# The last head of each layer routed for two tiles on one load, and gathers handled in groups of two picks

## The chip, the cores and the metric

One core of one Trainium2 chip runs the whole program in a single launch. The metric is device time in microseconds (us), on the only core, as a median of runs. Below, TensorE, VectorE, ScalarE, GpSimd and SyncE stand in the profile as PE, DVE, ACT, POOL and SP.

## What is computed

Two layers of a decoder trunk over 256 tokens of width 1024, all float32. Each layer first mixes tokens (attention with a forget gate, a pooling mixer and a state-space mixer beside each other), then applies a retrieval layer (PEER) over 16384 experts. The second part, cut to what matters here:

```python
def peer_ffn(h, w_q, sub_keys, u_tab, v_tab):
    q = einsum('bsd,de->bse', h, w_q).reshape(bsz, s, 8, 2, 128)
    scores = einsum('bshid,hikd->bshik', q, sub_keys)
    top_s, top_i = top_k(scores, 16)                      # for each half
    cand = top_s[..., 0, :, None] + top_s[..., 1, None, :]
    best_s, best_j = top_k(cand.reshape(..., 256), 16)
    experts = i1 * 128 + i2                               # 16 for each of 8 heads
    gates = softmax(best_s)
    act = gelu(einsum('td,tkd->tk', hh, u_tab[experts]))
    return einsum('tk,tkd->td', gates * act, v_tab[experts])
```

So every token needs 8 x 16 = 128 experts, and each expert is a row of 1024 numbers of u and 1024 of v (8 KB).

## The kernel before, in words

The 256 tokens are two tiles of 128, one token in each partition. With two layers that makes four steps (STEPS): steps 0 and 1 are tiles 0 and 1 of layer 0, steps 2 and 3 those of layer 1. A **pick** is one of a token's 128 experts. For each pick `gather` has POOL issue one indirect DMA, which brings 128 rows of 8 KB into one of SLOTS = 13 slots (L583). DVE multiplies the u half with the token's activations and sums (`dots`, L1427). ACT applies Gelu and the gate and scales a small diagonal matrix with the result (`weigh`, L931, L938, L947). PE multiplies this diagonal with the v half into PSUM (`add_last`, L1830). Only then is the slot free, and POOL, which waits for `expert_done`, issues the gather that is 13 picks further on.

Picks go in groups of GRP = 4 (a "quad", QUADS = 32 in a step). `dots` of a group run at its `open`, `weigh` at its `close`, and PE adds a group at the `close` of the following one.

While the picks of step n are worked off, the engines also compute the token mixing of step n + 1 and its **routing**. Routing one head takes: `rp`, 16 matmuls of the query projection (L1752); a copy by ACT (L890); `route`, two matmuls for the scores (L1791); a copy by ACT (L917); and on DVE two rounds of top 16 that end with the expert numbers (L1392) and the gates (L1365); `soft` on ACT is the softmax in between. All engines follow one list, `ORDER`, built by `script()`: the rows of MIX, MIX1 and ROUTES are dealt out evenly over the quads of the step before them, `while at < len(rows) * (quad + 1) // QUADS`. In step 0 there are 33 rows for 32 quads, so quad 31 has two: route6 and route7 of tile 1. MIX0 is the order of the start, before any expert can be gathered.

The weights come in blocks (chunks). The 12 blocks of tile 0's token mixing lie in the slots at first. All others pass through a ring of two buffers (`RING`, L518 on SP); the block for c waits until block c - 2 has been used. A routing block holds a head's projection and keys, 1152 KB. Each tile loads its own: RING has 60 blocks. `hT` holds the transposed activations that `rp` reads; step n + 1 overwrites them.

```python
            for c, (n, i) in enumerate(RING):
...
                if c >= 2:
                    sp.wait_ge(S["chunk_used"], uses(*RING[c - 2]))
                w = width(i)
                sp.dma_start(ring[:, c % 2, 0:w], weights[n // TILES, i, :, 0:w])
```

Of the kernel before, what the change touches and what calls it, by code (L numbers as in the profile page):

```python
# [23 lines left out]
P = 128  # L24
# [18 lines left out]
GRP = 4  # L43
# [21 lines left out]
for _name, _w in (("g1", 8), ("fbias", 1), ("qg", 1), ("kg", 1), ("pscale", 2), ("dskip", 2), ("glub", 2), ("og", 8),  # L65
# [40 lines left out]
ROUTES = tuple((f"route{h}",) for h in range(1, PH))  # L106


def script():
# [6 lines left out]
    for n in range(STEPS):  # L116
        if n == 0:

            rows = [(1, r) for r in ((), ("qkn",), ("qkT", "v"))]
            rows += [(0, r) for r in ROUTES[1:]] + [(1, r) for r in MIX1]  # L120
        else:
            rows = [(n + 1, r) for r in MIX + ROUTES] if n + 1 < STEPS else []
# [14 lines left out]
    for quad in (QUADS, QUADS + 1):  # L137
        order += [("open", n, quad), ("close", n, quad)]
# [11 lines left out]
def chunk_order():  # L150
# [7 lines left out]
    return order  # L158


USES = chunk_order()
RING = [c for c in USES if not in_slot(*c)]


# [1804 lines left out]
```

## Time and profile before

| | |
|---|---|
| time, median of 3 runs | 1546.36 us (1545.2 to 1547.12) |
| the profiled execution's own time | 1547.98 us |
| its span, first to last instruction | 1546.1 us |
| busy in the span: PE, DVE, ACT, POOL | 68%, 70%, 37%, 40% |
| moved by DMA | 623.55 MB, of these 536.90 MB by the gathers' queue |
| mean granted TensorE clock | 0.826 of 2.4 GHz |

The profile names an instruction by its line, its engine, what it writes and reads, and gives busy time, the mean length and the idle time of the engine just before it. A group of rows by stretch gives, from left to right, the stretch, its length, the busy time of PE, of PE's weight loads, of DVE, ACT and POOL, each with the count of instructions, then the granted clock, the busy share of the 16 DMA engines (it can pass 1 a little) and the GB/s they moved.

### The profile page before, as it was taken

The page shows a single profiled execution, that of the slowest core. Times are in us where ns is not written, and L with a number is a line of the kernel's source. Part 1 is how long each engine was busy: PE and PEld are TensorE (multiplying, and loading weights), DVE is VectorE, ACT ScalarE, POOL GpSimd, SP SyncE. Part 2 cuts the span into 40 slices and gives each one's busy share as a digit, 9 for nine tenths or more (in the row PEclk, how much of TensorE's full clock was granted, in tenths as well). Part 3 has the DMA queues.
Part 4 walks back from the last instruction along what each step waited for, and adds up shares of the span by engine and source line. Part 5 has one row for each costly group of instructions (what it writes and reads, how often), then busy time and mean ns, then how long its engine had stood idle before and what let it go on. Part 6 is the DMA issues. An engine that isn't in the chain of part 4 may idle for free. (4 is left out here: it accounts for less than half of the span.)

```text
span 1546.1 us, 19439 instructions
## 1 busy us (share of the span) xinstructions
PE 1049.1 (68%) x6790; PEld 532.8 (34%) x6790; DVE 1083.2 (70%) x2485; ACT 575.1 (37%) x1768; POOL 619.7 (40%) x571
## 2 busy tenths in 40 slices
PE   8898656785854668776775667788588465565555
PEld 6685312333531334332552334333255111111111
DVE  8777998646999685654789767564579965444444
ACT  5544433623444433441544431354234432221222
POOL 0034345442753533443343433444243354455441
PEclk9999877887986988787897788889698777667767
DMA  9289999999999999999999999999999999999997
GB/s 381 89 326 421 420 421 420 421 421 405 422 421 368 411 422 421 421 421 421 409 421 421 421 421 421 421 422 420 422 386 421 421 421 422 421 421 422 421 421 304
DMA packets 86642, 623.55 MB, mean 403 GB/s; under 512 B 10000, under 2 KB 10128, under 8 KB 11792
## 3 DMA queue, kind: packets, MB, share of 16 engines
q0 software_dynamic: 73728, 536.90, 83.7%
q1 hardware_dynamic: 12816, 85.41, 13.4%
q8 instruction: 53, 0.87, 0.2%
q14 instruction: 45, 0.37, 0.1%
HBM read 621.23 MB, written 1.05 MB: 402 GB/s over the span
## 5 line engine op out<-in xcount | busy, mean ns | idle before, releaser
L583 POOL DMA_INDIRECT slots<-experts,idx x512 | 593.2, 1159 | 886.5 <-PE psum L1830 709.9
L1427 DVE CUSTOM_DVE_ANT_0 slots<-slots,h 128x1024 f32<-128x1024 f32 x512 | 615.9, 1225 | 390.8 <-DMA slots<-experts,idx 387.6
L1830 PE MATMUL psum<-slots,diag 64*64 64x512 f32 x4088 | 599.3, 737 | 312.4 <-ACT diag L947 312.3
L1830 PEld LDWEIGHTS psum<-slots,diag 64*64 64x64 f32 x4088 | 175.8, 165 | 684.2 <-ACT diag L947 368.9
L931 ACT ACTIVATE ge<-ge 128x4 f32<-128x4 f32 x130 | 26.7, 205 | 437.3 <-DVE ge L1427 436.3
L1752 PE MATMUL psum<-hT,ring 128*128 128x128 f32 x992 | 131.3, 297 | 20.7 <-DMA ring<-weights 16.0
L931 ACT ACT_TABLE_LOAD x55 | 70.6, 1283 | 194.7 <-DVE ge L1427 194.3
L947 ACT ACTIVATE diag<-cst,ge 128x64 f32<-128x64 f32 x511 | 136.5, 336 | 6.7 <-PE psum L1830 2.5
L1752 PEld LDWEIGHTS psum<-hT,ring 128*128 128x128 f32 x992 | 127.7, 212 | 23.5 <-issue 17.7
L938 ACT ACTIVATE ge<-ge,gate 128x1 f32<-128x1 f32 x512 | 109.1, 283 | 4.2
L1525 PE MATMUL psum<-ring,hT 128*128 128x256 f32 x192 | 52.2, 433 | 17.5 <-DVE work L981 17.5
L1525 PEld LDWEIGHTS psum<-ring,hT 128*128 128x128 f32 x192 | 41.1, 220 | 31.3 <-DVE work L981 19.2
L1699 PE MATMUL psum<-ring,work 128*128 128x512 f32 x96 | 44.4, 605 | 0.0
L1427 DVE DVE_READ_ACCUMULATOR2_ANT ge<- 128x1 f32 x512 | 42.1, 82 | 0.0
L925 ACT ACT_TABLE_LOAD x30 | 38.5, 1283 | 0.5
L1791 PE MATMUL psum<-ring,work 128*128 128x128 f32 x124 | 22.5, 305 | 15.8 <-ACT work L890 15.8
L890 ACT COPY work<-psum 128x256 f32<-128x256 f32 x31 | 11.5, 372 | 58.2 <-PE psum L1752 54.6
L809 ACT ACT_TABLE_LOAD x12 | 15.4, 1283 | 43.4 <-DVE att_s L1232 43.4
L1791 PEld LDWEIGHTS psum<-ring,work 128*128 128x128 f32 x124 | 16.6, 194 | 40.4 <-ACT work L890 22.1
L1738 PE MATMUL psum<-cst,h 128*128 128x128 f32 x24 | 5.9, 427 | 30.7 <-DVE h L1295 30.7
L1699 PEld LDWEIGHTS psum<-ring,work 128*128 128x128 f32 x96 | 17.3, 190 | 24.8 <-issue 24.8
L1539 PE MATMUL psum<-work,c_bar 128*32 128x128 f32 x64 | 5.0, 386 | 28.6 <-DVE work L981 28.6
(292 smaller groups left out, 1075.4 us busy)
## 6 DMA issues: line engine op xcount, KB each, us to landing
ring<-weights SPq DMA_DIRECT2D x32, 1152.0 KB, 10.0
ring<-weights SPq DMA_DIRECT2D x26, 1024.0 KB, 9.2
slots<-weights SPq DMA_DIRECT2D x11, 1024.0 KB, 20.0
slots<-experts,idx POOLq DMA_INDIRECT x512, 20.8
ring<-weights SPq DMA_DIRECT2D x2, 1056.0 KB
sml<-small SPq DMA_DIRECT2D x2, 652.0 KB, 9.1
slots<-weights SPq DMA_DIRECT2D x1, 1056.0 KB, 9.0
xs<-x SPq DMA_DIRECT2D x2, 512.0 KB, 13.2
```

The costliest lines, as they stand in the source:

```text
L583: pool.indirect_dma_start(out=slot[:, place(E), :], out_offset=None, in_=src, in_offset=bass.IndirectOffsetOnAxis(ap=idx[:, n % 2, e:e + 1 ...
L809: told(act.activation(prob[:, h % 2, 0:w], PX[:, h % 2, 0:w], ACT.Exp, bias=att_s[:, 0, h:h + 1], accum_out=att_s[:, 1, h:h + 1]), "exp_re ...
L925: told(act.activation(bs[:, 1, :], bs[:, 0, :], ACT.Exp, bias=rs[:, 0:1], accum_out=rs[:, 1:2]), "gexp_ready")
L931: told(act.activation(ge[:, 1, G % 2, :], ge[:, 0, G % 2, :], ACT.Gelu_apprx_tanh), "gelu_ready")
L938: ins = act.activation(ge[:, 2, G % 2, i:i + 1], ge[:, 1, G % 2, i:i + 1], ACT.Copy, scale=gate[:, n % 2, e:e + 1])
L947: act.activation(diag[:, d % DIAGS, :], c_("fold"), ACT.Copy, scale=ge[:, 2, G % 2, i:i + 1]).then_inc(S["diag_ready"], 1)
L1427: ins = dve.tensor_tensor_reduce(u, u, h2[:, n % 2, :], 1.0, 0.0, ALU.mult, ALU.add, d[:, i:i + 1])
L1525: ins = pe.matmul(bank[:, (i % 2) * 256:(i % 2) * 256 + 256], hT_(n)[:, k, :], c[:, k, :], start=(k == 0), stop=(k == KD - 1))
L1699: ins = pe.matmul(out_at(n, i)[:, half, :], merged(n, k), c[:, (k % 2) * D + half * 512:(k % 2) * D + half * 512 + 512], start=(k == first ...
L1752: ins = pe.matmul(PB[:, 2 + h % 2, i * P:i * P + P], c[:, k, i * P:i * P + P], hT[:, k, :], start=(k == 0), stop=(k == KD - 1))
L1791: ins = pe.matmul(PB[:, 2 + h % 2, 256 + i * P:256 + i * P + P], qTs[:, h % 2, i * P:i * P + P], raw[:, KD * 256 + i * P:KD * 256 + i * P ...
L1830: ins = pe.matmul(acc[HALF * half:HALF * half + HALF, i, :], diag[rows, d % DIAGS, :], slot[rows, place(E), D + half * 512:D + half * 512 ...
```

## The change

1. **Groups of two.** GRP is 2, so a step has 64 quads. The last two picks of the last step stay single as before.
2. **One load for two tiles.** Head 7 (SHARED) of the two tiles of a layer is routed one directly after the other from one block. `owner` names both by one ring entry, and `given_back` lets the buffer go after the second. RING has 58 blocks. So tile 0's head 7 is routed only after tile 1's token mixing, and tile 1's heads go in the order 7, 0, 1, ... 6. Both tiles' transposed activations must exist then, so odd steps keep theirs in the work buffer W[0] (`hR_`).
3. **Placing.** `rows_of` gives even steps a first part (until quad EARLY = 46: the rest of the own routing, the mixing of the next tile) and a second (9 routings in the last 18 quads). No quad has two routings.
4. **`adds`.** In front of the rows that hold one of FOLLOWS, PE adds the group that waits, instead of behind the row.
5. **The start.** MIX0 puts `qkn0` before `scan0`, halves `scan0` (`scan_im`), spreads `mul0` to `mul3`, and lets the projections `p`, `qkv0` and `qkv1` of tile 1 go ahead of `route1`. SP loads the block CH_Q before the constants.

```diff
-GRP = 4
+GRP = 2
...
-        "power4", "qkv0", "f", "prep", "fx", "ln", "mul0", "mul1", "mul2", "mul3", "rotate0", "rotate1", "cum", "cm",
-        "qkv1", "rotate2", "bu", "qkv2", "scan0", "qkv3", "qkn0", "scan1", "qkn1", "qkv4", "pool", "qkT", "pre0", "pre1",
...
+        "power4", "qkv0", "f", "prep", "fx", "ln", "mul0", "rotate0", "rotate1", "cum", "cm", "mul1", "mul2",
+        "qkv1", "rotate2", "bu", "qkv2", "qkv3", "qkn0", "scan0", "qkn1", "scan_im", "qkv4", "pool", "qkT", "pre0", "pre1",
+        "mixp", "mul3", "sq1", "scan1", "scan2", "scan3", "scan4", "scan5", "scan6", "logits0", "scan7", "big0", "logits1",
...
+SHARED = (7,)
+OWN = tuple(h for h in range(PH) if h not in SHARED)
+EARLY = (TOPK * SHARED[0] - SLOTS - 7) // GRP
+FOLLOWS = {"normT", "u", "qkv0", "y", "glu", "qkT", "att1", "att2", "att3", "att4", "out0", "h2T"}
+def rows_of(n):
+    if n == STEPS - 1:
+        return [], 0, QUADS
+    pair = [(n + i, h) for h in SHARED for i in range(2)]
...
+    if n % TILES:
+        rows = last_row(rows, n + 1, OWN[0]) + routing([(n + 1, h) for h in OWN])
+        return rows, len(rows), QUADS
+    rows = last_row(rows, n, SHARED[0])
+    late = routing(pair + [(n + 1, h) for h in OWN])
...
+    return rows + late, len(rows), EARLY
...
+                if FOLLOWS.intersection(row):
+                    order.append(("mix", "adds", n))
...
+def owner(n, i):
+    return (n - n % TILES, i) if i - CH_ROUTE in SHARED else (n, i)
-RING = [c for c in USES if not in_slot(*c)]
+RING = list(dict.fromkeys(owner(*c) for c in USES if not in_slot(*c)))
...
+def given_back(n, i):
+    return uses(n + 1, i) if i - CH_ROUTE in SHARED else uses(n, i)
...
+        def hR_(n):
+            return W[0][:, :].rearrange("p (a b) -> p a b", a=KD) if n % TILES else hT
...
             chunk(CH_POOL)
+            chunk(CH_Q)
             sp.dma_start(cst[:, P:], consts[:, P:]).then_inc(S["cst_in"], 16)
...
-                    sp.wait_ge(S["chunk_used"], uses(*RING[c - 2]))
+                    sp.wait_ge(S["chunk_used"], given_back(*RING[c - 2]))
...
+            def adds(n):
+                add_last()
```

How the order moves, at the places that matter. First PE at the end of tile 1's token mixing in step 0, where `out0` to `out3` are L1699, the transposes of `h2T` are L1738, `rp` L1752 and `route` L1791. Before:

```order
160 L1699 MATMUL psum<-ring,work 128x512 x4
161 L1830 MATMUL psum<-slots,diag 64x512 x16
162 L1699 MATMUL psum<-ring,work 128x512 x4
163 L1830 MATMUL psum<-slots,diag 64x512 x16
164 L1738 MATMUL psum<-cst,h 128x128 x8
165 L1752 MATMUL psum<-hT,ring 128x128 x16
166 L1830 MATMUL psum<-slots,diag 64x512 x16
167 L1791 MATMUL psum<-ring,work 128x128 x2
168 L1752 MATMUL psum<-hT,ring 128x128 x16
169 L1830 MATMUL psum<-slots,diag 64x512 x16
```

With the change, the same place (`out3` L1763, `h2T` L1802, `rp` L1814, `route` L1854, adding L1891; a pick is four matmuls in this list, and eight in the profile, which counts each float32 matmul twice):

```order
159 L1763 MATMUL psum<-ring,work 128x512 x4
160 L1891 MATMUL psum<-slots,diag 64x512 x16
161 L1763 MATMUL psum<-ring,work 128x512 x4
162 L1891 MATMUL psum<-slots,diag 64x512 x16
163 L1802 MATMUL psum<-cst,h 128x128 x8
164 L1814 MATMUL psum<-hT,ring 128x128 x16
165 L1891 MATMUL psum<-slots,diag 64x512 x8
166 L1854 MATMUL psum<-ring,work 128x128 x2
167 L1814 MATMUL psum<-work,ring 128x128 x16
```

Between `out3` and `h2T` there are now the adds of two groups of two, up to the group just weighed, where before the group of four weighed during `out3` was added behind `rp`.

Then PE at the end of step 0. Before, and behind it with the change:

```order
183 L1752 MATMUL psum<-hT,ring 128x128 x16
184 L1830 MATMUL psum<-slots,diag 64x512 x16
185 L1791 MATMUL psum<-ring,work 128x128 x2
186 L1752 MATMUL psum<-hT,ring 128x128 x16
187 L1791 MATMUL psum<-ring,work 128x128 x2
188 L1830 MATMUL psum<-slots,diag 64x512 x48
```

```order
187 L1854 MATMUL psum<-ring,work 128x128 x2
188 L1814 MATMUL psum<-work,ring 128x128 x16
189 L1891 MATMUL psum<-slots,diag 64x512 x16
190 L1854 MATMUL psum<-ring,work 128x128 x2
191 L1891 MATMUL psum<-slots,diag 64x512 x48
```

The two `route` with no adds between them (185 and 187 of before) are apart now. Last, DVE at the start, where L1187 is `qkn0`, L1122 the scans, L1210 `big0`, and the rows of 128x1024 around them `scan0` and `qkn1`. Before:

```order
95 L981 TENSOR_TENSOR work<-psum,rot 128x1024 x2
96 L981 TENSOR_TENSOR work<-work,ring 128x1024
97 L981 TENSOR_TENSOR work<-work 128x1024
98 L1187 TENSOR_REDUCE ssqk<-work 128x16
99 L1122 SCALAR_TENSOR_TENSOR work<-decay,work 128x128 x2
100 L1192 RECIPROCAL ssqk<-ssqk 128x16
101 L981 TENSOR_TENSOR work<-psum,ssqk 128x1024
102 L1122 SCALAR_TENSOR_TENSOR work<-decay,work 128x128 x12
103 L1210 TENSOR_REDUCE att_s<-psum 128x4
```

With the change:

```order
95 L1041 TENSOR_TENSOR work<-psum,rot 128x1024 x2
96 L1251 TENSOR_REDUCE ssqk<-work 128x16
97 L1041 TENSOR_TENSOR work<-work,ring 128x1024
98 L1256 RECIPROCAL ssqk<-ssqk 128x16
99 L1041 TENSOR_TENSOR work<-psum,ssqk 128x1024
100 L1041 TENSOR_TENSOR work<-work 128x1024
101 L1186 SCALAR_TENSOR_TENSOR work<-decay,work 128x128 x14
102 L1274 TENSOR_REDUCE att_s<-psum 128x4
```

The normalised queries and keys are written by the instruction numbered 99 now, with one 128x1024 pass and two scans fewer ahead of it.

## Rows read from the trace of the kernel before

**Rows 1.** The page: GB/s in 40 equal slices of the span.

```profile
GB/s 381 89 326 421 420 421 420 421 421 405 422 421 368 411 422 421 421 421 421 409 421 421 421 421 421 421 422 420 422 386 421 421 421 422 421 421 422 421 421 304
```

**Rows 2.** The page: all DMA traffic.

```profile
DMA packets 86642, 623.55 MB, mean 403 GB/s; under 512 B 10000, under 2 KB 10128, under 8 KB 11792
```

**Rows 3.** By stretch: the places with less than full rate; columns as explained above.

```profile
42.00:90.00 48.00, 45.99 (x302) 35.54 (x301) 35.19 (x84) 27.84 (x71) 2.99 (x3) 0.96 0.22 79
376.00:396.00 20.00, 17.64 (x151) 12.08 (x154) 15.22 (x44) 7.66 (x27) 8.30 (x8) 0.99 0.96 392
466.00:476.00 10.00, 7.49 (x44) 2.79 (x48) 9.72 (x33) 4.24 (x13) 4.39 (x4) 0.69 0.70 267
498.00:512.00 14.00, 11.99 (x99) 6.47 (x92) 13.79 (x25) 9.15 (x31) 10.85 (x8) 0.95 0.94 360
750.00:756.00 6.00, 6.00 (x57) 3.81 (x50) 4.14 (x16) 2.53 (x11) 4.18 (x4) 1.00 0.94 365
1122.00:1136.00 14.00, 14.00 (x116) 8.99 (x115) 9.89 (x34) 6.03 (x23) 5.99 (x6) 0.93 0.85 322
1526.00:1546.10 20.10, 10.81 (x72) 2.93 (x64) 10.39 (x16) 4.74 (x19) 0.00 (x0) 0.75 0.48 198
```

**Rows 4.** The page, DMA issues: the routing blocks.

```profile
ring<-weights SPq DMA_DIRECT2D x32, 1152.0 KB, 10.0
```

**Rows 5.** Timeline of the end of tile 1's mixing in step 2: PE (two), POOL.

```profile
1118.20 6.63 PE L1752 MATMUL psum<-hT,ring 128*128 128x128 f32 x32 [1.56 <-ACT hT L880]
1124.76 3.67 PE L1830 MATMUL psum<-slots,diag 64*64 64x512 f32 x32
...
1126.15 1.44 POOL L583 DMA_INDIRECT slots<-experts,idx  x1 [19.66 <-PE psum L1830]
```

**Rows 6.** Timeline: when ACT has the waiting group's diagonals there.

```profile
1116.00 1.06 ACT L947 ACTIVATE diag<-cst,ge 128x64 f32<-128x64 f32 x4
```

**Rows 7.** Timeline of the end of step 0: PE (two), POOL.

```profile
466.66 1.23 PE L1791 MATMUL psum<-ring,work 128*128 128x128 f32 x4 [8.66 <-ACT work L890]
467.82 5.79 PE L1830 MATMUL psum<-slots,diag 64*64 64x512 f32 x32
...
470.11 0.97 POOL L583 DMA_INDIRECT slots<-experts,idx  x1 [13.12 <-PE psum L1830]
```

**Rows 8.** Timeline of DVE: the expert numbers of two consecutive routed heads.

```profile
454.27 0.18 DVE L1392 SCALAR_TENSOR_TENSOR idx<-ex 128x16 uint32<-128x16 f32 x1
467.22 0.17 DVE L1392 SCALAR_TENSOR_TENSOR idx<-ex 128x16 uint32<-128x16 f32 x1
```

**Rows 9.** Gathers issued in 1160 to 1170, 1220 to 1230, 470 to 475: issue to landing.

```profile
DMA to landing us min/median/max: 26.5/28.2/29.1
...
DMA to landing us min/median/max: 13.0/17.6/18.1
...
DMA to landing us min/median/max: 5.5/6.3/9.6
```

**Rows 10.** Timeline of the start: DVE (three), PE (two), ACT.

```profile
18.54 0.25 DVE L981 TENSOR_TENSOR rot<-phase,cst 128x8 f32<-128x8 f32 x2
40.10 1.23 DVE L981 TENSOR_TENSOR work<-psum,ssqk 128x1024 f32<-128x1024 f32 x1
48.01 0.69 DVE L1210 TENSOR_REDUCE att_s<-psum 128x4 f32<-128x512 f32 x1 [2.04 <-PE psum L1601]
...
41.38 1.36 PE L1560 MATMUL psum<-cst,work 128*128 128x128 f32 x8 [3.28 <-DVE work L981]
46.71 1.71 PE L1601 MATMUL psum<-kT,qT 64*128 64x128 f32 x16
...
36.20 1.02 ACT L755 ACTIVATE work<-psum 128x1024 f32<-128x1024 f32 x1
```

**Rows 11.** The page, costliest groups: the Gelu of a group.

```profile
L931 ACT ACTIVATE ge<-ge 128x4 f32<-128x4 f32 x130 | 26.7, 205 | 437.3 <-DVE ge L1427 436.3
```

**Rows 12.** Timeline of the end: DVE's final additions.

```profile
1540.66 3.05 DVE L978 SCALAR_TENSOR_TENSOR xs<-slots,ge,psum 64x512 f32<-64x512 f32 x4 [0.71 <-PE psum L1830]
```

More of the change, by code:

```diff
@@ L103, with routing, last_row @@
         ("att3", "max3", "nrm3"), ("att4", "attg", "sq"), ("merge", "out0"), ("out1", "x1a"),
[2 rows of a table removed]
-ROUTES = tuple((f"route{h}",) for h in range(1, PH))
+        ("out2", "x1p"), ("out3", "x1"), ("h2T",))
+SHARED = (7,)
+OWN = tuple(h for h in range(PH) if h not in SHARED)
+EARLY = (TOPK * SHARED[0] - SLOTS - 7) // GRP
+FOLLOWS = {"normT", "u", "qkv0", "y", "glu", "qkT", "att1", "att2", "att3", "att4", "out0", "h2T"}
+def routing(heads):
+    rows = []
+    for (n, h), ahead in zip(heads, heads[1:] + [None]):
+        rows.append((n, (f"route{h}",) + ((("rp%d" % ahead[1], ahead[0]),) if ahead else ())))
+    return rows
+def last_row(rows, n, h):
+    step, row = rows[-1]
+    return rows[:-1] + [(step, row + ((f"rp{h}", n),))]
+def rows_of(n):
+    if n == STEPS - 1:
+        return [], 0, QUADS
+    pair = [(n + i, h) for h in SHARED for i in range(2)]
+    if n == 0:
+        rows = [(1, r) for r in ((), ("qkn",), ("qkT", "v"))]
+        rows += routing([(0, h) for h in OWN[2:]]) + [(1, r) for r in MIX1]
+    else:
+        rows = [(n + 1, r) for r in MIX]
+    if n % TILES:
[3 more added lines that the diff above has]
+    late = routing(pair + [(n + 1, h) for h in OWN])
+    if n == 0:
+        late = [(step, row + ((f"tab{5 + i - 4}", TILES),) if 4 <= i < 7 else row) for i, (step, row) in enumerate(late)]
+    return rows + late, len(rows), EARLY
 def script():
@@ L116, in script @@
     for n in range(STEPS):
[L117 to L122, printed above, removed]
+        rows, early, until = rows_of(n)
         at = 0
@@ L128, in script @@
             done = at
-            while at < len(rows) * (quad + 1) // QUADS:
+            due = (early * (quad + 1) // until if quad < until else
+                   early + (len(rows) - early) * (quad + 1 - until) // (QUADS - until))
+            while at < due:
                 step, row = rows[at]
-                order += [("mix", s, 2 if s[:3] == "tab" else step) for s in row]
+                if FOLLOWS.intersection(row):
+                    order.append(("mix", "adds", n))
+                order += [("mix", s, step) if type(s) is str else ("mix",) + s for s in row]
                 at += 1
@@ L136, in script @@
                 order += [("mix", "soft" + s[5:], step) for s in row if s[:5] == "route"]
-    for quad in (QUADS, QUADS + 1):
-        order += [("open", n, quad), ("close", n, quad)]
-    return order + [("mix", "drain", STEPS - 1)]
+    return order + [("open", n, QUADS), ("close", n, QUADS), ("mix", "drain", STEPS - 1)]
 ORDER = script()
@@ L158, in chunk_order, with turn_of, routes_before @@
     return order
+def owner(n, i):
+    return (n - n % TILES, i) if i - CH_ROUTE in SHARED else (n, i)
 USES = chunk_order()
-RING = [c for c in USES if not in_slot(*c)]
+RING = list(dict.fromkeys(owner(*c) for c in USES if not in_slot(*c)))
+RSEQ = [(b, int(a[5:])) for kind, a, b in ORDER if kind == "mix" and a[:5] == "route"]
+def turn_of(n, h):
+    return RSEQ.index((n, h))
+def routes_before(stage):
+    return sum(1 for kind, a, b in ORDER[:ORDER.index(stage)] if kind == "mix" and a[:5] == "route")
+def given_back(n, i):
+    return uses(n + 1, i) if i - CH_ROUTE in SHARED else uses(n, i)
 FREE = CH_POOL
@@ L191, in experts_of @@
     start, end = PICKS * n + GRP * quad, PICKS * n + GRP * quad + GRP
-    if start >= PICKS * STEPS:
-        alone = PICKS * STEPS - 2 + quad - QUADS
-        return range(alone, alone + 1)
-    return range(start, min(end, PICKS * STEPS - 2))
+    last = PICKS * STEPS - 1
+    return range(start, min(end, last)) if start <= last else range(last, last + 1)
 BY_VECTOR = {PICKS * STEPS - 1}
@@ L495, in _ @@
             rest_(0)
-            for i in range(6):
+            for i in range(1, 6):
                 chunk(CH_Q + i)
@@ L906, in route @@
             def route(n, h):
-                R = PH * n + h
+                R = turn_of(n, h)
                 if R == 0:
@@ L1116, in scan @@
                     link(tt(w3[0], w3[0], spare, ALU.add))
-                    link(tt(w3[1], w3[1], w3[3], ALU.subtract))
+                if part == 9:
+                    scan_im(n)
                 todo = [(r, b) for r in range(2) for b in range(SB)]
```

58 lines of the change are left out of this document (28 added, 30 removed), and 18 rows, old and new, of tables (MIX, MIX0, MIX1).

## The prediction

> **What bounds the kernel now.** The first view to read is the page's line of GB/s by slice [rows 1]. In most of the 40 slices it stands at 420 to 422, and it never stays above. That is what the DMA engines can do with this traffic, so the kernel is bound by bytes wherever this line is full. At 421 GB/s the 623.55 MB of [rows 2] take 1481 us. The profiled execution took 1547.98 us around a span of 1546.1 us, 1.6 us above the median of the runs, 1546.36 us; I make the sum in differences and take them off the median.
>
> So the second question is where the DMA engines are not full, since only that and the bytes can give time back. The stretches answer it [rows 3]. Each loses its length times (421 - GB/s) / 421. The start, 42 to 90 us, loses 48 x 342 / 421 = 39.0 us: the first weights are in, and no expert can be fetched before the first head is routed. The end loses 20.1 x 223 / 421 = 10.6 us. Between them lie five holes: 1.4 us at 376, 3.7 at 466, 2.0 at 498, 0.8 at 750 and 3.3 at 1122, together 11.2 us. With 1481 that is 1542 of the 1546 us; the rest is mostly the ramp of the first 20 us.
>
> The third view is the timeline at the holes. Those at 376, 750 and 1122 are one pattern. In the last one POOL issues no gather for 19.66 us [rows 5], as no slot comes free: the diagonals of the waiting group of four are there from 1116.0 on [rows 6], but PE works in order and has `h2T` and `rp` first, and `rp` takes 6.63 us at the low clock. The adds follow at 1124.76, the gather at 1126.15. The hole at 466 is another: PE stands 8.66 us before `route` of the doubled quad, while a group of four waits behind it, and then adds at the low clock for 5.79 us [rows 7]. The hole at 498 follows from the second routing of that quad, which keeps DVE from the dots.
>
> **The change, part by part.**
>
> *Bytes.* Two routing blocks of 1152 KB, 1.18 MB each [rows 4], are no longer loaded: 2.36 MB / 421 GB/s = 5.6 us. This counts in full if the DMA engines stay full around it. If VectorE is the bound in those two stretches it counts nothing, which is the other end: 0 to 5.6. I take 5.6, since the line was at 421 through the routing stretches at 1160 to 1240 as well [rows 1].
>
> *The three holes at `h2T`*, 1.4 + 0.8 + 3.3 = 5.5 us. Now PE adds the two groups of two before the transposes, as soon as ACT has the diagonals, so at about 1117 and not 1124.8 in the case of [rows 5, 6]: gathers resume some 8 us sooner and the pause of 19.66 us shrinks to about 12. The hole of 3.3 us needs only 3.3 of these 8. Late next is `h2T`, by the 3.7 us of the adds, and so `rp`; behind `rp` two to four picks wait again. Head 7's `route` stands two quads later, about 5 us, so VectorE doesn't wait for it. I keep 0.5 us of hole: minus 5.0 us (bounds 0 and 5.5).
>
> *The two holes of the doubled quad*, 3.7 + 2.0 = 5.7 us. No quad has two routings now, and every second quad has none, so PE meets adds of two picks between them. In the second hole the DMA share was 0.94 at 360 GB/s, so engines were busy but moved less: the small tables of layer 1 come there, and they still do. I leave 1.5 us: minus 4.2 us (bounds 0 and 5.7).
>
> *The start.* Until the first gather everything hangs on DVE's queue. DVE writes the normalised queries from 40.10 on, PE transposes them at 41.38, has the logits from 46.71 on, and DVE stands 2.04 us until 48.01 [rows 10]. The scan pass and two scans that were ahead go behind, so qkn_ready comes one 128x1024 pass (1.23 us) and two scans of 128 columns (0.74 us) sooner, 2.0 us. The scans that fill the time until the logits are the same work, so DVE's standing goes away, and all behind moves by 2.0 us. ACT must have the squares when DVE is through with `bu`, which is 40.10 less three passes of 1.23, the two scans and a reciprocal, so at 35.4. It began them at 36.20 and took 1.02, behind 32 small multiplications of mul0 to mul3. Eight of them now come later, some 1.8 us, and `f`, which heads the chain, comes sooner with CH_Q loaded first, I take 1 us; so ACT begins at about 33.4 and ends at 34.4, in time. The constants move behind 1 MB, 2.5 us, and DVE first reads them at 18.54, with some us in hand. Tile 1's first projections go ahead of route1, which frees slots 6 to 8 sooner and delays nothing before pick 16. Minus 2.0 us (bounds: plus 1, where a load is late; minus 3).
>
> *A new cost: nine routings in a row.* A routing with its four dots takes DVE 467.22 - 454.27 = 12.95 us [rows 8]. DMA needs 4 gathers of 1.05 MB and a block of 1.18 MB for it, 12.8 us. They are nearly even. Now nine stand in a row in steps 0 and 2, and one of them has no block to load: 9 x 12.95 = 116.6 us of DVE against 112 of DMA. So VectorE falls behind by 4.6 us, where eight of before were behind by 1.5. What covers this is the queue of issued gathers. Its depth is the time from issue to landing [rows 9]: 28.2 us when routing begins at 1160, 17.6 at 1220, and 6.3 in a hole, where it is empty. Groups of two free slots earlier by about two picks' dots, 2.3 us, each time. I expect it to get shallow but seldom empty: plus 1.0 us (bounds 0 and 9, see the rivals).
>
> *More instructions.* ACT has 127 Gelus more, 205 ns each [rows 11], 26 us in all. ACT is 37% busy, and what hides them is the time in which DMA lands the next pick. In the routed stretches they are at most 18 x 0.2 = 3.6 us each on ACT, which isn't the late engine there. DVE and ACT hand over twice as often; between 0 and the same 0.2 us a group, inside the term above. Nothing.
>
> *SP and POOL.* The pair's buffer goes back a routing later, and the next load is wanted two quads after that, as before; at 10.0 us to landing [rows 4] it fits in the 12.95. POOL's three table pieces in step 0 stay behind routings. Nothing. *The end.* DVE's last additions start at 1540.66 [rows 12], after the single picks' last gate value; these stay single. Nothing.
>
> Sum: -5.6 - 5.0 - 4.2 - 2.0 + 1.0 = **-15.8 us**: 1530.6 us for the median (1532.2 for the profiled execution).
>
> **The rivals.**
>
> *B, VectorE drains the queue.* The queue lost 28.2 - 17.6 = 10.6 us in 60 us, 4.6 routings: 2.3 us each [rows 9]. Nine of them and the pair's missing block would take 20.7 + 2.8 = 23.5 of the 28.2 us, and leave 4.7, under the 6.3 of an empty queue. POOL's table work in step 0 and the drain behind both stretches come on top. About 4 us each, 8 in all: 1538.6 us. Against it speaks that last blocks of a layer aren't loaded in that fall, and that groups of two return slots sooner.
>
> *C, the sharing doesn't save what it says.* The block for (1, 0) is loaded late, behind the second use of the shared one, and PE stands before it for 2 us in each layer, or the start doesn't move: 4 us more, 1534.6 us. For: `given_back` is later by one routing. Against: the lead of one routing, 12.95 us, is unchanged.
>
> *D, smaller bursts keep TensorE at its low clock, and it becomes the bound.* At the low level `rp` takes 6.63 us, `route` 1.23 and four picks 5.79 [rows 5, 7], 13.65 us for a routing, against 12.8 us of DMA. Add a wait for the diagonals of two groups, half of the 1.06 us of four picks [rows 6] for each, and it is 14.7. Over the 25 routings that stand close (9 + 7 + 9) that is 25 x 1.9 = 48 us, less what three queues of about 9 us give: +21 beyond the forecast, 1552 us, slower than before. It decides from about 14.6 us a routing on: there 25 times the excess, less 27, eats the 15.8. Against: `rp` and adds still lie end to end, and the clock granted in the full stretches at 376 and 1122 was 0.99 and 0.93 [rows 3]. The Trainium skill has such a rule, in "TensorE: Matmul & The Clock Gate", section "HAM oscillation — how this bites in real kernels": bursts of matmuls that are shorter than the wait before them begin at half rate each time. By that rule the adds of this change, in half the size, would each start cold, and 1552 would be the time. The trace agrees in part: in the stretch of the lone burst at 467.82 the granted clock was 0.69 [rows 3].
>
> *E, nothing to see.* The holes come back elsewhere and VectorE's backlog eats the bytes too: within 3 us of 1546.4.
>
> **How the numbers follow.** The forecast has 0.64, B 0.18, C 0.07, D 0.06, E 0.05. The predicted time is that of the likeliest, 1530.6 us. Its own bounds reach down to 1526 (all holes gone, 3 us at the start) and up to 1535. To hold 8 in 10 the range goes to 1540, which takes in B and C with their spread and leaves out D and E. A measurement here can tell 0.2%, 3.1 us. Faster by more than that are the forecast, B and C, 0.89; within it E, 0.05; slower D, 0.06.
>
> **What would show it.** DMA traffic of 621.2 MB. 421 GB/s in all slices after the third. No pause of POOL over 15 us at the three `h2T`, and landing times that stay over 8 us at the ends of the two long routing stretches. The first gather at 84.3 and not 86.3 us. The forecast is wrong if DVE shows 99% busy there beside DMA slices under 400 (B), if PE stands before L1814 for a block (C), or if a routing takes PE over 13 us (D).

## The result and the profile after

The changed kernel takes **1549.76 us** (median of 20 runs, 1547.69 to 1552.14), the kernel before 1546.36 us beside it (20 runs, 1545.2 to 1548.04): a ratio of 1.002, 95% interval 1.0013 to 1.0027, so 3.4 us more. Forecast were 1530.6 us, and 1525.5 to 1540.0 as range. The profiled execution took 1551.14 us around a span of 1549.3 us.

The page of the changed kernel, bytes, and GB/s by slice, to be held against [rows 1, 2]:

```profile
GB/s 378 91 335 421 420 421 421 386 403 421 421 398 332 423 420 421 421 421 421 422 420 421 420 421 421 421 420 406 421 421 421 412 374 422 421 421 421 421 421 314
DMA packets 86357, 621.22 MB, mean 401 GB/s; under 512 B 9968, under 2 KB 10096, under 8 KB 11760
```

The bytes are the forecast's to the tenth. But the line isn't full: there are dips in slices 8, 9, 12, 13, 28, 32 and 33. The stretches of the changed kernel (start to end, length, busy time and count of PE, PEld, DVE, ACT and POOL, granted PE clock, DMA share, GB/s):

```profile
42.00:90.00 48.00, 45.90 (x294) 35.18 (x293) 36.45 (x86) 29.17 (x78) 3.46 (x4) 0.97 0.25 87
270.00:320.00 50.00, 36.70 (x230) 15.12 (x226) 28.32 (x58) 29.05 (x78) 17.80 (x18) 0.84 0.95 380
376.00:396.00 20.00, 12.03 (x100) 8.08 (x102) 18.22 (x53) 9.72 (x26) 14.46 (x29) 0.92 1.01 422
470.00:500.00 30.00, 14.00 (x80) 4.52 (x84) 27.70 (x85) 12.63 (x35) 7.78 (x8) 0.64 0.80 308
750.00:756.00 6.00, 5.14 (x40) 2.44 (x33) 3.07 (x5) 2.19 (x6) 4.57 (x4) 0.90 1.01 419
1122.00:1136.00 14.00, 10.67 (x88) 6.80 (x90) 12.90 (x44) 7.36 (x21) 3.90 (x4) 0.91 1.01 420
1220.00:1260.00 40.00, 24.44 (x160) 7.19 (x152) 38.18 (x88) 17.68 (x55) 15.39 (x15) 0.72 0.91 366
1526.00:1549.30 23.30, 11.79 (x56) 2.76 (x56) 11.62 (x18) 5.15 (x20) 0.00 (x0) 0.65 0.59 244
```

Three of these places in the kernel before, which [rows 3] doesn't have:

```profile
270.00:320.00 50.00, 40.04 (x235) 18.82 (x232) 32.82 (x65) 30.42 (x84) 20.23 (x19) 0.86 1.01 421
470.00:500.00 30.00, 10.53 (x76) 3.18 (x72) 29.01 (x87) 11.91 (x31) 9.59 (x9) 0.68 0.96 387
1220.00:1260.00 40.00, 19.09 (x140) 5.59 (x136) 33.54 (x76) 13.41 (x45) 20.11 (x18) 0.79 1.01 421
```

The ledger below (us) has each kernel's bytes at 421 GB/s and, by stage, the length times (421 - GB/s) / 421 of stretches of 10 us, added up. Bytes and losses give the span by arithmetic, whatever the kernel. So the ledger says where a span is lost, and not that an edit which closes a hole makes the span shorter by as much. The experiments below are read by it too, each in its one profiled execution, which can lie some 2 us off the median (that of the changed kernel 1.4 above, that of the kernel without `adds` 2.3 below).

| | bytes | start, to 90 | attention rows | `h2T` rows | routing, 400 to 520 | routing, 1150 to 1300 | tail, from 1500 | span |
|---|---|---|---|---|---|---|---|---|
| before | 1481.1 | 42.7 | 0 | 5.6 | 5.7 | 0 | 10.7 | 1546.1 |
| changed | 1475.6 | 42.1 | 6.4 | 0.1 | 10.2 | 5.1 | 9.8 | 1549.3 |
| forecast's change | -5.6 | -2.0 | 0 | -5.0 | -3.2, both routing stretches | | 0 | |

So two terms came in the size forecast (the bytes; the holes at `h2T`, 376, 750 and 1122, which are full now), and two things went against the sum: 6.4 us at the attention rows, which the forecast did not look at, and 9.6 us more in the two long routing stretches, where it had 3.2 us less.

**The attention rows.** Timeline of the changed kernel around two rows of attention of step 1 (computed during step 0) (start, us, engine, line, operation; in brackets the idle time ahead and who ended it), PE, ACT and DVE:

```profile
293.16 5.36 PE L1891 MATMUL psum<-slots,diag 64*64 64x512 f32 x32 [3.61 <-ACT diag L1007]
...
299.04 0.70 PE L1644 MATMUL psum<-kT,qT 64*128 64x256 f32 x2
...
294.66 0.59 ACT L1007 ACTIVATE diag<-cst,ge 128x64 f32<-128x64 f32 x2
...
287.75 0.42 DVE L1296 TENSOR_REDUCE att_s<-psum 128x1 f32<-128x256 f32 x1 [4.05 <-PE psum L1646]
...
295.06 1.22 DVE L1491 CUSTOM_DVE_ANT_0 slots<-slots,h 128x1024 f32<-128x1024 f32 x1
...
300.52 0.43 DVE L1296 TENSOR_REDUCE att_s<-psum 128x1 f32<-128x256 f32 x1 [4.23 <-issue]
```

Here the new step `adds`, put ahead of each row that FOLLOWS names, makes a ring of three engines. PE does not start on the logits (L1644) before it has added both waiting groups (L1891, until 298.5); for that it needs ACT's diagonals (the second group's until 295.25), and ACT needs DVE's dots, the last of which, for the group after, ends at 296.3. DVE's next work is the maximum of those logits (L1296), and behind it stand the next dots. DVE is idle 4.23 us in front of it (the profile names no releaser for this wait; the one a turn earlier it puts to PE). One turn is 300.52 - 287.75 = 12.77 us for four picks, which DMA brings in 4 x 1.05 MB / 421 GB/s = 10.0 us. The other turns, between the rows of L1296, are 10.6 and 12.5 us in step 1, and 13.8 and 13.7 us in step 3. They are 13.4 us over DMA in all, of which the gathers already issued hide about half. In the kernel before the logits went ahead of the adds, and PE did them while DVE was at the dots. The view of waits of the changed kernel, DVE (us in all, times, longest), has what the kernel before hardly has (no wait of its maximum for PE on its list, and 2.2 us for `xs`):

```profile
DVE slots L1491 <- DMA slots<-experts,idx: 232.7, 177, 3.9
DVE att_s L1296 <- PE psum L1646: 38.1, 19, 5.4
DVE xs L1038 <- PE psum L1763: 21.0, 9, 4.6
```

and the kernel before waited most for what an engine at the bytes' bound should wait for:

```profile
DVE slots L1427 <- DMA slots<-experts,idx: 387.6, 278, 4.0
```

**The routing stretches.** The expert numbers of consecutive heads in the changed kernel, as in [rows 8], and what ACT does between two of them:

```profile
1183.65 0.17 DVE L1456 SCALAR_TENSOR_TENSOR idx<-ex 128x16 uint32<-128x16 f32 x1
...
1189.77 0.49 DVE L1377 MAX8 ts<-work 128x8 f32<-128x128 f32 x2 [0.65 <-ACT work L979]
...
1197.36 0.17 DVE L1456 SCALAR_TENSOR_TENSOR idx<-ex 128x16 uint32<-128x16 f32 x1
...
1186.79 1.28 ACT L991 ACT_TABLE_LOAD   x1 [4.54 <-DVE ge L1491]
1188.08 0.20 ACT L991 ACTIVATE ge<-ge 128x2 f32<-128x2 f32 x1
1188.32 0.48 ACT L998 ACTIVATE ge<-ge,gate 128x1 f32<-128x1 f32 x2
1188.83 0.59 ACT L1007 ACTIVATE diag<-cst,ge 128x64 f32<-128x64 f32 x2
1189.32 0.35 ACT L979 COPY work<-psum 128x256 f32<-128x256 f32 x1
```

A routing takes DVE 13.71 us, and not 12.95. The copy of the scores (L979), by which the next routing starts, now stands on ACT behind the weighing of a group of two whose dots DVE has just done; the Gelu's table load is in it. DVE has four dots, one every 1.15 us, from 1184.33 to 1189.1 and then waits 0.65 us for that copy. DVE has no other wait over 0.5 us in 1220 to 1260 and is busy 38.18 of the 40 us, beside 366 GB/s.

**The start.** The first gather goes out at 85.63 us, where it was 86.26:

```profile
34.15 1.28 ACT L815 ACT_TABLE_LOAD   x1 [1.86 <-PE psum L1589]
35.45 1.02 ACT L816 ACTIVATE work<-psum 128x1024 f32<-128x1024 f32 x1
...
36.57 1.22 DVE L1251 TENSOR_REDUCE ssqk<-work 128x16 f32<-128x1024 f32 x1 [1.46 <-ACT work L816]
...
85.63 1.12 POOL L644 DMA_INDIRECT slots<-experts,idx  x1 [67.49 <-DVE idx L1038]
```

ACT's square starts at 35.45 and not at 33.4: it had been idle 1.86 us for PE's projection (L1589), and then loads a table. DVE, which got there sooner as forecast, stands 1.46 us for it.

### The profile page after: what moved, and what is told of

Read it like the earlier page. It is cut to its first block, busy times and chain, and to the rows that moved or that the text cites. A ratio compares the mean times of both kernels' runs of the same rounds, so it can differ in the third digit from the quotient of the medians.

```text
span 1549.3 us, 19844 instructions
## 1 busy us (share of the span) xinstructions
PE 1066.3 (69%) x6790; PEld 501.2 (32%) x6790; DVE 1080.6 (70%) x2485; ACT 627.9 (41%) x1897; POOL 582.6 (38%) x571
## 3 DMA queue, kind: packets, MB, share of 16 engines
HBM read 618.87 MB, written 1.05 MB: 400 GB/s over the span
## 4 chain that ended last, share of the span: by engine, by line
DMA 24%; DVE 11%; PE 8%; ACT 4%; issue 4%; POOL 1%; another core or an unknown queue 0%; ACTq 0%; DVEq 0%
DMA slots<-experts,idx 23%; PE psum L1891 5%; DVE slots L1491 3%; DVE work L1041 2%; ACT L991 1%; DVE work L1379 1%; POOL slots L644 1%; ACT diag L1007 1%; PE psum L1763 1%; DMA ring<-weights 1%; ACT ge L998 1%; DVE ex L1455 1%; PE psum L1589 1%; DVE ti L1389 0%; DVE ti L1387 0%
## 5 line engine op out<-in xcount | busy, mean ns | idle before, releaser
L1891 PE MATMUL psum<-slots,diag 64*64 64x512 f32 x4088 | 652.7, 779 | 450.0 <-ACT diag L1007 428.7
L644 POOL DMA_INDIRECT slots<-experts,idx x512 | 552.0, 1078 | 918.6 <-PE psum L1891 755.0
L1891 PEld LDWEIGHTS psum<-slots,diag 64*64 64x64 f32 x4088 | 170.0, 166 | 868.8 <-ACT diag L1007 621.0
L991 ACT ACTIVATE ge<-ge 128x2 f32<-128x2 f32 x257 | 52.1, 203 | 442.8 <-DVE ge L1491 398.8
L998 ACT ACTIVATE ge<-ge,gate 128x1 f32<-128x1 f32 x512 | 123.0, 287 | 8.4
L1814 PE MATMUL psum<-hT,ring 128*128 128x128 f32 x480 | 60.9, 289 | 8.5 <-DMA ring<-weights 7.6
L1814 PEld LDWEIGHTS psum<-hT,ring 128*128 128x128 f32 x480 | 59.2, 205 | 9.4 <-issue 8.3
L1814 PE MATMUL psum<-work,ring 128*128 128x128 f32 x512 | 59.9, 275 | 0.4 <-DMA ring<-weights 0.4
L1814 PEld LDWEIGHTS psum<-work,ring 128*128 128x128 f32 x512 | 58.5, 192 | 0.6 <-issue 0.6
L1763 PE MATMUL psum<-ring,work 128*128 128x512 f32 x96 | 45.1, 613 | 0.6 <-DMA ring<-weights 0.6
L1296 DVE TENSOR_REDUCE att_s<-psum 128x1 f32<-128x256 f32 (+1 forms) x24 | 9.1, 380 | 42.5 <-PE psum L1646 38.1
L1377 DVE MAX8 ts<-work 128x8 f32<-128x128 f32 x64 | 15.7, 286 | 29.8 <-ACT work L977 15.0
L1038 DVE SCALAR_TENSOR_TENSOR xs<-psum,rn,xs 128x1024 f32<-128x1024 f32 (+1 forms) x13 | 15.6, 1202 | 21.2 <-PE psum L1763 21.0
L1763 PEld LDWEIGHTS psum<-ring,work 128*128 128x128 f32 x96 | 17.6, 194 | 26.5 <-issue 26.5
L1854 PEld LDWEIGHTS psum<-ring,work 128*128 128x128 f32 x124 | 16.4, 192 | 26.4 <-issue 26.4
## 6 DMA issues: line engine op xcount, KB each, us to landing
sml<-small SPq DMA_DIRECT2D x2, 652.0 KB, 13.7
xs<-x SPq DMA_DIRECT2D x2, 512.0 KB, 13.5
```

The lines of the kernel that those rows point to most:

```text
L644: pool.indirect_dma_start(out=slot[:, place(E), :], out_offset=None, in_=src, in_offset=bass.IndirectOffsetOnAxis(ap=idx[:, n % 2, e:e + 1 ...
L991: told(act.activation(ge[:, 1, G % 2, :], ge[:, 0, G % 2, :], ACT.Gelu_apprx_tanh), "gelu_ready")
L998: ins = act.activation(ge[:, 2, G % 2, i:i + 1], ge[:, 1, G % 2, i:i + 1], ACT.Copy, scale=gate[:, n % 2, e:e + 1])
L1377: step(dve.max(vals[:, 0:8], src))
L1763: ins = pe.matmul(out_at(n, i)[:, half, :], merged(n, k), c[:, (k % 2) * D + half * 512:(k % 2) * D + half * 512 + 512], start=(k == first ...
L1814: ins = pe.matmul(PB[:, 2 + R % 2, i * P:i * P + P], c[:, k, i * P:i * P + P], hR_(n)[:, k, :], start=(k == 0), stop=(k == KD - 1))
```

## The experiments

Theory 1 (A in the expectations): the step `adds` costs the attention rows their overlap. Theory 2 (B in the expectations, which is not the prediction's rival B): the score copy behind a group's weighing makes the routing longer, and VectorE falls behind over nine of them. Rivals: groups of two as such; the shared block; the clock; the start. Medians are each beside runs of the kernel before on the same chip (1546.4 to 1546.7). The changed kernel was timed in its own set of runs only, and the differences from it below are taken from its 1549.76 us.

**No `adds` ahead of rows.**

```diff
-FOLLOWS = {"normT", "u", "qkv0", "y", "glu", "qkT", "att1", "att2", "att3", "att4", "out0", "h2T"}
+FOLLOWS = set()
```

> The changed kernel with FOLLOWS empty: PE adds no group ahead of a row any more. Theory A (the adds ahead of the attention rows make DVE wait for PE, PE for ACT and ACT for DVE, so four picks take 12.5 us there): the holes at 270 to 320 and 1040 to 1080, 6.3 us together, go, the wait of DVE before L1296 falls from 4 us to about 1, and the time falls by 4 to 6 us to about 1545. Theory B (only the routing stretches matter, where a head takes DVE 13.7 us and nine stand in a row): those attention holes come from a queue that was drained before, so they stay, and the time stays at 1549 to 1550. Either way POOL's long pauses at h2T may come back, up to plus 5 us.

Measured: 1542.21 us (1539.89 to 1543.46), 0.9973 of before (0.9963 to 0.9983). That is 7.6 us less than the changed kernel, and some 4 us less than before: theory 1, and more than the 4 to 6 us expected. Stretches and a wait of this kernel:

```profile
270.00:320.00 50.00, 41.17 (x254) 16.94 (x251) 28.01 (x51) 26.23 (x73) 23.16 (x22) 0.93 1.01 421
1122.00:1136.00 14.00, 10.30 (x68) 5.78 (x68) 12.90 (x41) 6.65 (x18) 4.07 (x4) 0.76 1.01 421
1220.00:1260.00 40.00, 26.05 (x184) 7.19 (x176) 33.54 (x74) 15.83 (x55) 20.48 (x19) 0.80 0.90 359
...
DVE att_s L1296 <- PE psum L1646: 7.0, 9, 0.9
```

The loss at attention is gone, and DVE's wait for PE there with it (38.1 us in the changed kernel). That of the routing at 1220 is not gone (the two routing stretches lose 12.1 us in the ledger, after 15.3); and the holes at `h2T` do not come back, though `adds` was what the forecast had them closed by.

**The score copy first.** ACT copies the scores ahead of the weighing of the group that closes before the routing:

```diff
...
             def weigh(n, quad):
                 G = QUADS * n + quad
+                at = ORDER.index(("close", n, quad))
+                if ORDER[at + 1][0] == "open":
+                    for kind, a, b in ORDER[at + 2:]:
+                        if kind != "mix":
+                            break
+                        if a[:5] == "route":
+                            route(b, int(a[5:]))
...
```

The lines left out keep `route` from copying the same scores twice.

> The changed kernel, but ACT copies a head's scores before it weighs the group of the quad ahead, which has no routing. Theory B: DVE no longer waits for that copy (0.65 us of each routing), expert numbers follow each other by about 13.05 us instead of 13.70, the holes at the ends of the two long routing stretches shrink from 15.5 us to 4 to 8, and the time falls to 1540 to 1543. Theory A: the cycle may shorten, but the time falls by 2 us at most, as the queue comes into the stretch drained.

Measured: 1544.09 us (1543.35 to 1545.17), 0.9979 (0.997 to 0.9989): 5.7 us less than the changed kernel. The numbers of the heads of this kernel come every 13.06 to 13.15 us:

```profile
1202.06 0.17 DVE L1468 SCALAR_TENSOR_TENSOR idx<-ex 128x16 uint32<-128x16 f32 x1
1215.12 0.17 DVE L1468 SCALAR_TENSOR_TENSOR idx<-ex 128x16 uint32<-128x16 f32 x1
```

Some 0.6 us a routing is gone. Its ledger loses 7.1 and 1.7 us in the two routing stretches, against 10.2 and 5.1; also 2.8 us at the attention rows, against 6.4, though their code is the same, and 13.6 us in the tail, against 9.8. Theory 2 is borne out by the period, which was expected at 13.05 us. The time missed its 1540 to 1543 us by 1.1 us.

**Both.** The two edits together.

> The changed kernel with both: no adds ahead of rows, and ACT's copy of the scores ahead of the empty quad's weighing. Alone they gave 7.5 and 5.7 us. If the two losses are separate places (A at the attention rows, B in the routing stretches) they add up but for what the drained queue shared: 1536 to 1539. If they were one loss (a queue that either of them keeps from emptying): no better than the better one, 1541 to 1543.

Measured: 1540.5 us (1539.38 to 1541.25), 0.9961 (0.9947 to 0.9975). The two gains are 7.6 and 5.7 us one by one, which would be 13.2, and 9.3 us together, between the two outcomes that were expected. The ledger shows a part of the loss as shared: each edit also took some 3 us of holes out of the other's place (3.2 us of the routing holes went without `adds`, 3.6 us of the attention holes with the early copy). Its profiled span, 1538.1 us, is that of the kernel without `adds` alone; the holes are fewer by 5.2 us in the routing stretches, and the tail is longer by 4.2 us (more on this in the last section).

**`adds` ahead of `h2T` alone**, without the early copy and with it (FOLLOWS = {"h2T"}).

> The change with `adds` only ahead of the rows with `h2T`. Theory (the harm is at the attention rows): as without any `adds`, 1542, the holes of 290 and 1050 gone, those of the two long routing stretches there with 12 us together. Rival (the harm is ahead of any row, also `h2T`, as the groups are added before their turn): between 1542 and 1549, nearer 1546.

> The early score copy, and `adds` only ahead of the rows with `h2T` (FOLLOWS = h2T alone). Theory (with groups of two the holes at `h2T` are gone by themselves, and the `adds` do harm only at the attention rows): the same as with the early copy and no `adds`, 1540.5, within 1 us; no hole over 1 us at 376, 750 and 1122. Rival (it is the `adds` ahead of `h2T` that close these holes, and without them something is lost): 2 us less than 1540.5, 1538.5.

Measured: 1543.26 us (1541.73 to 1544.72), 0.9981 (0.9972 to 0.999), and 1540.22 us (1538.99 to 1541.89), 0.9961 (0.9947 to 0.9974). The first is 1.1 us over its counterpart without any `adds`, with intervals that overlap, and the second 0.3 us under its own. So on groups of two the step shows no gain at `h2T`, and nearly all the harm is in the other rows; harm of about 1 us at `h2T` is not excluded.

**Groups of four again**, with `adds` and without (GRP = 4; the second also FOLLOWS = set()).

> The changed kernel with groups of four. Each quad of a stretch has a routing, so no copy stands behind an empty quad and a head takes 12.95 us of DVE again. The adds ahead of rows stay. Theory A and B: the attention holes stay or grow (a group of four waits there for PE), the routing holes shrink: 1545 to 1549. If groups of two are what hurts: under 1542.

> Groups of four again (GRP = 4) and no `adds` ahead of rows (FOLLOWS empty); sharing, start and queues as in the change. Theory 1 (the `adds` cost 5 us at the attention rows, groups of two cost a longer routing, 13.70 instead of 12.95 us): the attention holes of 290 and 1050 are gone, the period of head routings is 12.95 us, about 1541 us. Rival (the `adds` were needed where groups are of four, because a group's diagonals wait behind `h2T` and the projection): the holes at 376, 750 and 1122 of the kernel before come back with 4 to 5 us, and the time stays at 1545. Rival 2 (groups of two do the main work, only the attention rows hurt): no better than the same without `adds` on groups of two, 1542.

Measured: 1545.51 us (1540.87 to 1547.99), 0.9989 (0.9979 to 1.0), and 1549.4 us (1547.1 to 1551.77), 1.0017 (1.0008 to 1.0026). The routing is 12.96 us long with `adds` (1152.46 to 1165.42) and loses 0.4 us in the second stretch, but 7.3 in the first, and attention 8.0. Without `adds` attention loses nothing, and the routing 7.7 and 2.3 us, but a new hole of 8.0 us opens at step 1's `h2T`. PE and POOL of this last kernel:

```profile
355.63 1.97 PE L1802 MATMUL psum<-cst,h 128*128 128x128 f32 x8 [19.04 <-DVE h L1359]
357.39 4.76 PE L1814 MATMUL psum<-hT,ring 128*128 128x128 f32 x32
362.07 3.66 PE L1891 MATMUL psum<-slots,diag 64*64 64x512 f32 x32
...
363.47 0.94 POOL L644 DMA_INDIRECT slots<-experts,idx  x1 [28.76 <-PE psum L1891]
```

PE stands 19 us before the transposes, a group of four behind it, and POOL has no slot for 28.76 us. So the 1541 us expected of theory 1 were wrong. Its rival was right in kind: with groups of four the kernel with `adds` is 3.9 us the faster, as the step saves at `h2T` the 8.0 us that it costs at attention, and the routing stretches lose 2.3 us less with it. The rival had the size and the place wrong: it expected 1545 us and holes at all three `h2T`, and at the other two only 0.3 and 0.5 us are lost.

**Groups of two alone.** The kernel before, with GRP = 2 (and the ranges of the last group, which follow from it).

> The kernel before with groups of two and nothing else (at the end the last two picks stay single). The quad with two routings is gone by this too. Theory B: a head again takes 13.7 us of DVE, since ACT's copy of the scores stands behind an empty quad's weighing; holes at 466 and 498 (5.7 us) go, new ones of 3 to 6 us come at the ends of the routing stretches: 1545 to 1548. If smaller groups are good in themselves (slots free sooner): under 1542. If their handovers cost: over 1550.

Measured: 1546.69 us (1546.17 to 1549.94), 1.0005 (0.9994 to 1.0016): no difference, as theory 2 expected (1545 to 1548). Two stretches of this kernel:

```profile
1122.00:1136.00 14.00, 11.46 (x87) 8.12 (x84) 11.11 (x38) 5.05 (x16) 7.11 (x8) 0.91 1.01 421
1220.00:1260.00 40.00, 22.45 (x160) 6.44 (x164) 35.26 (x77) 17.41 (x57) 17.50 (x16) 0.83 0.90 357
```

It closes the holes at `h2T` (5.6 us in the ledger to 0) and the first routing stretch gains 1.8 us, and it opens the second, where before lost nothing, by 6.1 us. Its routings are 13.69 us long, as in the changed kernel. It has no sharing and no `adds`, so the longer routing comes of the group size alone.

**No sharing.**

```diff
-SHARED = (7,)
+SHARED = ()
...
-EARLY = (TOPK * SHARED[0] - SLOTS - 7) // GRP
+EARLY = QUADS - 2 * PH
...
-    rows = last_row(rows, n, SHARED[0])
+    rows = last_row(rows, n + 1, OWN[0])
```

> The changed kernel without sharing: each tile loads its own block for head 7, eight routings stand in a row and not nine, 623.6 MB. Theory B with the nine in a row as a large part: 5.6 us more of bytes, but the backlog of a stretch falls from 11 to 7.5 us, so the holes in the routing stretches fall from 15.5 to about 8 us: 1547 to 1549. If instead sharing really saves its bytes in full: plus 5.6 us, 1555.

EARLY is 48 here. Measured: 1554.48 us (1553.98 to 1557.71), 1.0057 (1.0035 to 1.0079); 623.58 MB. Sharing is worth 4.7 us by the medians, of the 5.6 that its bytes take. Theory 2 had expected 1547 to 1549, and that the ninth routing in the row eats most of the bytes; it does not. The ledger without sharing loses 12.9 us in the routing stretches, against 15.3. With four runs and an interval of 3.4 us on either side, this doesn't tell 5.6 from 3.

**The old start.** MIX0 in its old order up to the first scans, and CH_Q loaded behind the constants. Tile 1's first projections stay ahead of `route1`.

> The changed kernel with the old order of the start up to the attention's first scores, and CH_Q behind the constants. By the traces the new order moved the first gather by 0.6 us only (86.26 to 85.63): plus 0.6 us, 1550. By the prediction it was worth 2.0 us: plus 2.

Measured: 1552.45 us (1551.1 to 1554.63), 1.0043 (1.0028 to 1.0058): the new start is worth 2.7 us by the medians, with an interval of 2.3 us on either side of this kernel's own (four runs). In the trace the first gather is at 86.58 us, 0.95 later than in the changed kernel; over the kernels with the new start it lies between 84.3 and 86.1, so one profiled execution does not size this. What the other 1.7 us are stays open.

**Routing spread out.** Both edits, and EARLY = 42, so that the shared routing begins earlier in its step.

> e8_both with EARLY 42 in place of 46: nine routings over 22 quads and not 18, so 4.9 picks a routing; DVE then needs 14.1 us for what takes DMA 15.0. Theory B (nine in a row outrun the queue): the holes left at the ends of the stretches go too, 1534 to 1537. Against it: the mixing rows ahead get denser, 3.5 picks a row, and may drain the queue there: then 1538 to 1542.

Measured: 1540.27 us (1539.83 to 1541.93), 0.9963 (0.9949 to 0.9976): nothing beyond the two edits, where theory 2 expected 1534 to 1537 us. The first routing stretch loses 0.6 us less in the ledger, the second the same 3.6. Most of these 3.6 us lie behind the last routing, at the change of step: 1230 to 1240 stands at 302 GB/s in this kernel and in the one with both edits. PE stands 8.3 us there for DVE's additions to `xs` (L1053), the adds of the picks come behind, from 1230.71 on, and POOL has no slot for 9.73 us. So this last hole isn't one of nine routings in a row; no run tried it by itself.

## Why the prediction was wrong

**Bytes**: right. 2.33 MB went, 5.5 us at 421 GB/s, and taking the sharing out again costs 4.7.

**The three holes at `h2T`**: the size was right (0.1 us is left of 5.6), the reason was not. The prediction had "PE adds the two groups of two before the transposes" close them. Without `adds` on groups of two they stay closed (as with groups of two in the kernel before); with groups of four the step is needed. PE and POOL of the kernel with groups of two and without `adds`, at the same place of step 2:

```profile
1094.45 3.61 PE L1891 MATMUL psum<-slots,diag 64*64 64x512 f32 x16 [8.46 <-ACT diag L1007]
1097.99 1.09 PE L1802 MATMUL psum<-cst,h 128*128 128x128 f32 x8
...
1102.59 3.66 PE L1891 MATMUL psum<-slots,diag 64*64 64x512 f32 x32
...
1103.98 0.94 POOL L644 DMA_INDIRECT slots<-experts,idx  x1 [4.67 <-PE psum L1891]
```

PE adds a group of two (L1891) straight ahead of the transposes (L1802), and the four picks behind the projection at 1102.59. POOL pauses 8.11 us before the gather at 1096.74 and 4.67 us before that at 1103.98, where the kernel before had one pause of 19.66 us [rows 5]. In the changed kernel the longest pause at the three `h2T` is 8.11 us, where the prediction had about 12.

**The first step that failed is what is missing: `adds` was costed at one place only**, at `h2T`, as a gain. FOLLOWS names twelve steps, and ahead of each of them PE is made to wait for ACT's diagonals before work that DVE is waiting for. The prediction looked at PE for what `adds` delays at `h2T` ("late next is `h2T`, by the 3.7 us of the adds") and not at who waits for PE in the four attention rows. There the turn is 12.77 us against 10.0 of DMA. Price: 6.4 us in the ledger; 7.6 us when taken out, with 3.2 us of routing holes among what goes.

**The second is a term mis-sized, "nine routings in a row", +1.0 with bounds 0 and 9.** Its base, 12.95 us a routing, was read from groups of four and carried over; with groups of two it is 13.71. The prediction looked at what ACT does in addition ("127 Gelus more", 0.2 us each, nothing) and not at the order on ACT: a group's weighing with its table load now ends just when DVE wants the score copy. Nine times 13.71 against nine times 12.8 and a missing block is 11 us of backlog and not 4.6. The prediction had a second sign against its +1.0: the queue of issued gathers lost 2.3 us a routing in the kernel before, by rival B's own reading of [rows 9], where the sum allows for 0.15 (12.95 against 12.8). And a part of the loss lies at the change of step, behind the routings (last experiment above). This term, and the one for **the doubled quad's holes** (-4.2 for 5.7 us), which lie in the same stretch, should be one sum: -3.2 forecast, +9.6 measured. The hole at 498 did go: 498 to 512 stands at 420 GB/s now. Bigger ones than that of 466 took its place from 430 to 500.

**The start**: -2.0 forecast, -0.6 in the traces, -2.7 by the times of four runs; inside its bounds. The mechanism held on DVE, and its cover didn't: ACT's square hangs on PE's last projection, which the prediction had not traced back.

**More instructions: nothing.** Wrong in the sense above: the harm shown is that of the place in the queue, and nothing points at the count.

**The range.** The terms' own upper bounds add up to +10 us (0, 0, 0, +1 and +9), 1556 us, which would have held the result. The 1535 and 1540 us of the prediction don't come out of them.

**The rivals.** B had the place and nearly the mark (VectorE 99% busy beside slices under 400): 95% busy beside 366 GB/s in 1220 to 1260, 92% beside 308 in 470 to 500. Its price was 8 us over the forecast, and these two stretches came 12.8 us over it (+9.6 for -3.2). Its other mark, landing times, can't be read, as the changed kernel's profile has none. D's condition is met in part: the granted clock of the two routing stretches is 0.64 and 0.72 on the mean, between the levels of 1.2 and 2.4 GHz, and four picks' adds in the attention row above take 5.36 us and not 3.67 [rows 5]. But PE is busy 24.44 of 40 us there, some 8.4 us of a routing's 13.71, where D's mark was 13; and DVE is what is busy. The kernel with groups of two alone has the hole at 1220 at a higher clock (0.83, 357 GB/s) than the kernel before has there without one (0.79, 421 GB/s). So nothing points at the clock as the bound, though no run set it by itself. By the rule of the Trainium skill that D named (in "TensorE: Matmul & The Clock Gate", "HAM oscillation — how this bites in real kernels"), the bursts begin at half rate. The trace agrees in part, by these mean clocks. Its time of 1552 is 2.2 us from the measured one, and that is an accident. C did not happen: PE waits 8.1 us in all for a block at L1814, at most 2.8 at once, and waited 16.0 us at L1752 before. E missed by 0.4 us of time, less than the measurement can tell. Half of its sentence holds, the holes come back elsewhere; the other half doesn't, as the bytes were saved.

## What to carry to other kernels

A step that makes an in-order engine wait for a producer must be costed at every place where it is put, by who waits for that engine there; what it gains at one place is only one term. When a group size changes, no period read from the old size holds: trace the order on each engine that hands over inside the period again. And before the gain of an edit is put down to one of its parts, take that part out: here the holes at `h2T` were closed by the group size, and the part that was meant for them only cost. The best kernels of this study keep the sharing, the start and the groups of two, and leave `adds` out and copy the scores first: 1540.5 us and, with variants of it, 1540.2 and 1540.3, about 6 us under the kernel before.

## What the runs showed of the hardware

**The last gathers can hang on one DMA engine for 6 us.** The profiled execution of the kernel with the early copy (and `adds` only at `h2T`) has 6.8 us of holes in the routing stretches; that of the kernel without `adds` and without the early copy has 12.1. Their spans are 1538.4 and 1538.1 us (the second was the fastest of its runs; the medians are 2.0 us apart). Most of the difference sits in the tail, 13.7 and 9.3 us. The same stretch of both, with the early copy first, without second:

```profile
1524.00:1530.00 6.00, 3.59 (x24) 0.79 (x20) 3.33 (x6) 1.46 (x6) 0.00 (x0) 0.56 0.07 27
```

```profile
1524.00:1530.00 6.00, 2.98 (x24) 0.89 (x20) 2.96 (x6) 1.76 (x7) 0.00 (x0) 0.83 0.59 246
```

A share of 0.07 is one busy engine of 16. DVE's dots still wait there for a gather every 2.5 us (at 1525.94, 1528.54 and 1531.00), and 1.05 MB in 2.5 us would be the full 421 GB/s. In the trace, the gathers' packets of 8 KB come one behind another from 1524.5 to 1530.4, never two at once: eight of 0.31 us for each gather, 2.5 us. Eight of a gather's 128 rows are one engine's part of 16. So I read it that the last gathers wait for one engine, and that the others had brought their parts before; the trace gives no engine's number with a packet. In all four kernels with the early copy the packets run one at a time for the last 4.9 to 5.9 us, and their tails lose 13.5 to 14.0 us. With groups of four and no `adds` it is 3.7 us beside 12.4, and in the other eight kernels 0.6 to 2.2 us beside 9.1 to 11.3. What sets the engine back is open.

**A tiny VectorE operation can last 5.88 us.** It takes 0.17 us elsewhere. DVE and POOL of the changed kernel:

```profile
417.10 2.06 POOL L606 TENSOR_TENSOR work<-rot 128x512 f32<-128x512 f32 x2
417.75 5.88 DVE L1456 SCALAR_TENSOR_TENSOR idx<-ex 128x16 uint32<-128x16 f32 x1
419.11 2.04 POOL L606 TENSOR_TENSOR rot<-rot 128x512 f32<-128x512 f32 x2
421.12 2.47 POOL L606 TENSOR_TENSOR rot<-rot,work 128x512 f32<-128x512 f32 x2
423.66 0.19 POOL L656 COPY done_<-phase 128x8 f32<-128x8 f32 x1
```

It ends with the last of POOL's six table operations in a row. The Trainium skill, "SBUF — State Buffer", section "Who interferes with whom", says that a DVE instruction with two SBUF inputs contends with a GpSimd instruction that reads SBUF. The trace agrees: this operation has two such inputs (both halves of `ex`). It also goes further: the operation lasted through all that were left of six GpSimd instructions in a row. The kernel before has long operations beside the same table work too, a TENSOR_TENSOR of 6.56 us at 429.95 and a TENSOR_SCALAR of 2.85 at 420.01, so the change is not to blame for them; what they add to the first routing stretch was not tried by itself.
